# A gate multiplication of four coefficients moved to GpSimd, and VectorE's drain replaced by a wait, in the second pass of an expert mixer

## The reference

```python
def peer_ffn(h, w_q, sk1, sk2, eu, ev):
    q = (h @ w_q) ...                      # 8 heads, two halves of 128
    s1, s2 = scores of both halves against 128 keys each
    v1, i1 = lax.top_k(s1, 16); v2, i2 = lax.top_k(s2, 16)
    top_s, pos = lax.top_k(v1[..., :, None] + v2[..., None, :], 16)
    eidx = i1 * 128 + i2 at pos            # one of 16384 experts
    g = jax.nn.softmax(top_s, axis=-1)
    ...
        a = jax.nn.gelu(einsum('ckd,cd->ck', eu[it], ht)) * gt     # 128 experts of a token
        return jnp.einsum('ck,ckd->cd', a, ev[it])
```

## Time and profile before

| | us |
|---|---|
| median of 3 runs | 1510.64 (1509.07 to 1511.94) |
| the profiled execution, its own time | 1511.46 |
| its span, first to last instruction | 1509.6 |
| TensorE busy in the span | 1477.0 (98%) |
| VectorE busy | 1331.8 (88%) |
| ScalarE busy | 766.4 (51%) |
| GpSimd busy | 1022.5 (68%) |

### The profile page before, as it was taken

How to read it: one execution, slowest core, us unless ns; L and a number is a source line. 1 busy time by engine, 2 the same in 40 slices (tenths; PEclk the granted TensorE clock), 3 DMA queues, 4 the chain that set the end, 5 groups by cost and what they waited for, 6 DMA issues and landing times.

```text
span 1509.6 us, 21853 instructions
## 1 busy us (share of the span) xinstructions
PE 1477.0 (98%) x7296; PEld 1235.8 (82%) x7296; DVE 1331.8 (88%) x2235; ACT 766.4 (51%) x1181; POOL 1022.5 (68%) x732
## 2 busy tenths in 40 slices
PE   7999999999999999999989999999999999999997
PEld 5887778888887888888878888888888888888886
DVE  6497666687998999979969999999999999999998
ACT  4645442433545555554455555555555555555553
POOL 6643223333787777778877777777777777777773
PEclk8999999899999999999999999999999999999999
DMA  9335447222676898989989999999999999999994
GB/s 363 102 105 175 154 154 245 91 84 84 195 239 205 259 306 264 308 269 298 315 274 387 393 398 398 394 398 396 396 401 395 392 400 396 390 403 400 392 399 161
DMA packets 219582, 444.58 MB, mean 294 GB/s; under 512 B 22360, under 2 KB 128984, under 8 KB 219232
## 3 DMA queue, kind: packets, MB, share of 16 engines
q1 hardware_dynamic: 174432, 309.04, 57.7%
q0 software_dynamic: 45056, 134.38, 23.4%
HBM read 407.68 MB, written 35.67 MB: 294 GB/s over the span
## 4 chain that ended last, share of the span: by engine, by line
PE 90%; DVE 4%; DMA 3%; issue 1%; ACT 1%; DVEq 1%; POOL 0%; SPq 0%; ACTq 0%; POOLq 0%
PE ps L1831 15%; PE ps L1838 8%; PE ps L1804 8%; PE ps L1755 8%; PE ps L1807 8%; PE ps L1756 8%; PE ps L1757 8%; PE ps L1810 8%; PE ps L1504 4%; PE ps L1506 4%; PE ps L1505 4%; PE ps L1769 2%; DMA ada<-w_ada 2%; PE ps L1638 1%; PE ps L1590 1%; PE ps L1729 1%
## 5 line engine op out<-in xcount | busy, mean ns | idle before, releaser
L634 POOL TENSOR_TENSOR wlo<-raw,whi 128x1024 fp32r<-128x1024 f32 x178 | 428.8, 2422 | 294.2 <-ACT whi L713 294.0
L677 POOL DMA_INDIRECT rows<-w_stream,row_at x256 | 286.2, 1118 | 77.9 <-issue 77.9
L683 POOL DMA_INDIRECT coef<-gelu_spill,coef_at x256 | 279.8, 1093 | 79.9 <-issue 77.7
L713 ACT ACTIVATE whi<-raw 128x1024 fp32r<-128x1024 f32 x176 | 186.2, 1060 | 149.5 <-PE ps L1757 103.2
L1831 PE MATMUL ps<-acts,whi 128*128 128x512 f32 x1024 | 253.1, 389 | 0.0
L1831 PEld LDWEIGHTS ps<-acts,whi 128*128 128x128 f32 x1024 | 192.1, 188 | 40.4
L1755 PE MATMUL ps<-whi,acts 128*128 128x512 f32 x512 | 200.1, 391 | 2.8 <-DVE gate_lo L1336 2.2
L1756 PE MATMUL ps<-wlo,acts 128*128 128x512 f32 x512 | 199.6, 390 | 0.0
L1757 PE MATMUL ps<-whi,acts 128*128 128x512 f32 x512 | 199.2, 389 | 0.0
L1440 DVE SCALAR_TENSOR_TENSOR ps<-rows,coef,ps 128x1024 f32<-128x1024 f32 x126 | 162.4, 1289 | 11.2 <-issue 0.9
L1804 PE MATMUL ps<-whi,phi 128*128 128x512 f32 x512 | 161.7, 397 | 3.8 <-ACT phi L941 3.8
(11 more groups left out here) (252 smaller groups left out, 2585.7 us busy)
## 6 DMA issues: line engine op xcount, KB each, us to landing
raw<-w_stream SPq DMA_DIRECT2D x304, 512.0 KB, 5.8
values_in<-w_stream SPq DMA_DIRECT2D x128, 512.0 KB, 7.9
ada<-w_ada SPq DMA_DIRECT2D x32, 512.0 KB, 4.4
gelu_spill<-gout SPq DMA_DIRECT2D x64, 256.0 KB, 5.7
gate_spill<-gblock SPq DMA_DIRECT2D x8, 2048.0 KB, 10.2
gates<-gate_spill SPq DMA_DIRECT2D x32, 512.0 KB, 9.4
ada<-w_ada SPq DMA_DIRECT2D x32, 256.0 KB, 7.2
rows<-w_stream,row_at POOLq DMA_INDIRECT x256, 7.5
```

Source lines behind the costliest of these rows:

```text
L634: g.tensor_tensor(wlo[:, s, :], raw[:, s, :], whi[:, s, :].bitcast(F32), ALU.subtract)\
L677: g.indirect_dma_start(rows[m % ROWS][:, :], None, w_front.rearrange("c p n -> (c p) n"), bass.IndirectOffsetOnAxis(row_at[:, t * P + n:t ...
L683: g.indirect_dma_start(coef[:, t, n:n + 1], None, gelu_dram.rearrange("t p g (e o) -> (t p g e) o", o=1), bass.IndirectOffsetOnAxis(coef_a ...
```

## The change

```diff
+        coef_scaled = sem("coef_scaled")
+        gate_of_ready = sem("gate_of_ready")
...
+            def scale_coefs(b):
+                pool.wait_ge(coef_in[b % COEF_RING], 16 * PAIR * COEFS * (b // COEF_RING + 1))
+                some = slice(b * COEFS, (b + 1) * COEFS)
+                g.tensor_tensor(coef[:, :, some], coef[:, :, some], gate_of[:, :, some], ALU.mult).then_inc(coef_scaled, 1)
+
             for n in range(FIRST_ROWS, NK):
+                if n == 2 * COEFS:
+                    pool.wait_ge(gate_of_ready, 1)
+                if n >= 2 * COEFS and n % COEFS == 0:
+                    scale_coefs(n // COEFS - 1)
                 fetch_rows(n)
                 if n + FIRST_COEFS - FIRST_ROWS < NK:
                     fetch_coefs(n + FIRST_COEFS - FIRST_ROWS)
+            scale_coefs(NK // COEFS - 1)
...
             def add_row(n, t):
 
-                if t == 0:
-                    dve.drain()
-                    if n % COEFS == 0:
-                        scale_coefs(n // COEFS)
                 m = n * PAIR + t
+                if n >= 1:
+                    dve.wait_ge(row_added, m - 1)
+                if t == 0 and n == 0:
+                    scale_coefs(0)
+                elif t == 0 and n % COEFS == 0:
+                    dve.wait_ge(coef_scaled, n // COEFS)
                 dve.wait_ge(row_in[m % ROWS], 16 * (m // ROWS + 1))
...
-            v.tensor_copy(gate_of[:, :, :].rearrange("p t n -> p (t n)"), fetched[2])
+            v.tensor_copy(gate_of[:, :, :].rearrange("p t n -> p (t n)"), fetched[2]).then_inc(gate_of_ready, 1)
```

## The result

The changed kernel takes 1698.26 us (1697.87 to 1700.09, 4 runs) against 1511.29 us of the kernel before in the same session: ratio 1.1247, 95% interval 1.1231 to 1.1263. It is 187 us slower. The prediction said 1510.1 us and no measurable change, with 0.22 on slower and 1526 as the upper end of the range.

What follows compares the result with a forecast made beforehand. TensorE was taken to bound the second pass, VectorE and GpSimd close behind. Terms 0 + 0 - 0.58 + 0 gave -0.6 us on 1511.46, so 1510.9, or 1510.1 us for the runs' median; range 1508.3 to 1526.

Steps and rivals of the forecast that it cites:

- TensorE's 5.654 us a step: Second pass: TensorE sets the pace at 5.654 us a step, so relieving VectorE there is worth 0.
- The drain's 0.17 us: VectorE, ahead of `add_row(n, 0)`: replacing the drain by a wait saves 0.17 us a step, bounds 0 and 0.17.
- the spacing of 1.14 us: VectorE: subtraction to `ps` addition takes 1.14 us without the drain, against 1.31 us with it.
- The new instruction: GpSimd's 63 multiplications of 128x4: 0.13 us each plus 0.30 us of issue, 0.43 us for each two steps.
- The term for GpSimd: GpSimd, second pass: its multiplication comes out of existing lock waits, path cost 0 while total stays under 1.31 us.
- unlocks more time, not less: Argument against GpSimd becoming the bound: TensorE's pace leaves VectorE idle, which gives GpSimd more unlocked time.
- GpSimd becomes the bound: Rival at the new instruction and landing wait, ahead of the rows: slower by +14 to +59 us; chance 0.23.
- the landing wait: GpSimd waiting for its own coefficient fetches to land before multiplying: mostly none, at worst 0.7 us.
- the 1.31 us: GpSimd's supposedly free time in two steps: 11.31 us less the eight fetches' own 10.0 us.

Runs made afterwards that it cites:

- psum_both: Changed kernel with value and input chunk low parts made from PSUM sums, so neither long VectorE subtraction has two SBUF inputs (dense half wrong): 1510.07 us, ratio 0.9997.
- mult_drain_acc: Changed kernel plus a VectorE drain ahead of the addition to `acc`, multiplication still on GpSimd: 1510.38 us, ratio 0.9998 against the kernel before.
- no_mult2: Changed kernel's relieved VectorE without either drain, 63 of 64 coefficient multiplications and the first left out, nothing new on GpSimd: 1595.61 us, ratio 1.0573 against the kernel before.
- drain_only2: Changed kernel with the multiplication back on VectorE with its drain; only the wait on `row_added` replaces the drain ahead of additions: 1585.31 us, ratio 1.0513.
- mult_only2: GpSimd multiplies as in the changed kernel, but VectorE keeps its drain ahead of each first addition: 1559.05 us, ratio 1.0326 against the kernel before.
- psum_value_lo: Changed kernel with only the value chunk's low part made from the PSUM sum, from chunk 6 on (dense half wrong): 1557.4 us, ratio 1.0315.
- scale_ahead: Changed kernel with coefficients fetched two n further ahead and multiplied one group earlier: 1596.04 us, ratio 1.0562 against the kernel before.
- drain_value_lo: drain_only2 with a drain ahead of the value chunk's subtraction, multiplication on VectorE: 1512.75 us, ratio 1.0022 against the kernel before.

## Why the prediction was wrong

**What held.** That TensorE's 5.654 us a step leave nothing to gain from VectorE is what psum_both (VectorE relieved of drain and multiplication) and mult_drain_acc (relieved of the multiplication) show, both as fast as before. But GpSimd was as near to the bound as VectorE: it took 11.26 us for two steps (its coefficient fetches of 1202.51 and 1213.77 in the kernel before), against TensorE's 11.31. The drain's 0.17 us and the spacing of 1.14 us came out as said. The new instruction took 0.22 us (0.13 expected), and it adds less than 0.1 us to a round where I gave it 0.43.

**The step that failed** is the sentence on GpSimd: "They eat it only because GpSimd has time: a fetch that would come 0.4 us later meets the same instruction's end. I expect the new instruction to be taken out of those waits." GpSimd had no time to give: its gaps in the kernel before are the issue gaps alone, and its own work and 1.23 us of waits fill the 11.31 us of two steps. Nor are the waits a cushion in which anything fits. Each start depends on where the last fetch was let in, in steps of 1.12 or 1.25 us, and VectorE's instructions follow at distances of 1.14 and 1.19 us. Which fetch meets which start is decided by 0.01 to 0.02 us, and the price of a miss is a whole instruction. The term for GpSimd, "Cost on the path: 0", is 4.27 us of waits in two steps instead of 1.23, or 3.08 us for each of some 62 pairs.

**The second failure** is the drain at "0.17 saved", its work called worth nothing. I asked what its going is worth to VectorE, and not for whom the gap was good. It kept VectorE's and GpSimd's starts apart: taken out alone it costs 76 us. The prediction even said that VectorE's idle time would move, so that "the fetches fall on other instructions", and counted the idle time as a help ("unlocks more time, not less"); in no_mult2 the opposite happened.

**The rival** "GpSimd becomes the bound" named the mechanism (lock waits on GpSimd) and the sign, with 0.23. Its place was the new instruction and the landing wait, and there was no wait at either; the loss is in the fetches behind them. Its price was bounded too low, +14 to +59 us, for three reasons. It took the 1.31 us off as free, though today's waits of 1.23 us fill them. It let one wait of 1.22 us recur in two steps, where three long ones do (1.07 to 1.74 us). And it didn't have the loop: VectorE, waiting for the multiplication 63 times, is set going by it, so that the bad meeting comes back in each round. Rows that could have warned were there: a fetch of 1.78 us, and a GpSimd whose 78.36 us busy and 72 issue gaps of 0.30 us leave nothing of 100 us.

The rule of the Trainium skill, "SBUF — State Buffer", section "Who interferes with whom", was right where VectorE starts first: an instruction with one SBUF input stops no fetch and one with two does (0.95 us against 2.02). The other half that the prediction took from it, that a GpSimd instruction that starts first keeps the port to its end too, isn't what the traces show: in mult_drain_acc the subtraction of 1209.23 begins while the fetch of 1209.07 lasts and takes its usual 1.22 us.

**Where the 187 us are.** They are all in GpSimd's waits. The table sums, for the profiled execution of each kernel, what its fetches that start after 800 us took above 0.95 us, and sets it beside the time that this execution took longer than that of the kernel before.

| kernel | waits of the fetches, us | more than before | longer than before, us |
|---|---|---|---|
| before | 75 | | |
| changed | 260 | 185 | 186 |
| drain_only2 | 150 | 75 | 74 |
| mult_only2 | 123 | 48 | 48 |
| no_mult2 | 166 | 91 | 90 |
| psum_value_lo | 119 | 44 | 47 |
| scale_ahead | 150, and 11 of its multiplications | 85 | 88 |
| psum_both | 71 | -4 | -1 |
| mult_drain_acc | 58, and 14 of its multiplications | -3 | -3 |

So a microsecond more of waiting is a microsecond of time, because GpSimd had no idle time left. By the runs, about 86 us come with a VectorE relieved of drain and multiplication (no_mult2); about 100 more with its being released by the multiplication (scale_ahead against the changed kernel). The parts by themselves, 76 and 50, don't add up to it.

**Open.** Why a fetch that begins during the product is sometimes let in at its end (1.11 us, 0.12 to 0.14 us behind its start) and sometimes only two instructions later (2.69 and 2.50 us, 0.02 and 0.20 us behind it) no run tells. The distance alone doesn't decide it: the 60 fetches that start 0.01 to 0.03 us behind the product in the changed kernel all take 2.68 or 2.69 us, the 61 that do so in drain_value_lo all take 0.94 to 0.96, and there the product is stretched from 0.42 to 0.47 or 0.48 us instead. That is one reason why the fetches fit again in drain_value_lo; why they are let in there I did not find out.

## What to carry to other kernels

Before taking work or a drain from VectorE, see whether GpSimd is fetching in the same stretch and how close it is to being the bound; add its issue gaps to its busy time, as 78 us busy of 100 was no idle time at all here. Its fetches of 0.95 us were stretched to 2.7 by VectorE instructions with two inputs in SBUF, and a gap of 0.17 us on VectorE was worth 76 us. Free time that consists of lock waits is not free, and where two engines' starts repeat at a fixed distance, list those distances and ask which will change sign. Be wary of a handshake in which one engine's release comes from the other's in-order queue; it stands in mult_drain_acc too, at no cost, so if it can't be avoided, look for the one meeting that goes wrong and shift it.

## What was not expected of the hardware

An indirect DMA on GpSimd that started 0.01 to 0.02 us behind a VectorE subtraction of 128x1024 with both inputs in SBUF took 2.02 us, one that started 0.16 us ahead of it 1.07 us, and one behind the same subtraction with an input in PSUM 0.95 us. A fetch that waited ended 0.82 us (within 0.03) behind the end of a VectorE instruction, with hardly an exception in any of the traces. VectorE, in turn, hardly ever waited for a fetch: its product was stretched by up to 0.08 us (mult_drain_acc), and its value subtraction took 1.21 to 1.22 us in the kernel before with a fetch begun 0.3 us ahead of it. An explicit drain on VectorE cost 0.17 us. A 128x4 multiplication on GpSimd took 0.20 to 0.22 us where it met no long VectorE instruction, and 1.1 us once in scale_ahead, begun during the addition to `acc`.
